# Two heads' attention scores issued alternately in pairs, with their value products and endings reordered

## What is computed

```python
def banded_attention(q, k, v, slopes, sinks, max_delta, dist):
    # blocks of 128 queries against the previous and the own block of 128 keys
    s = jnp.einsum("nbqgrd,nbkgd->nbgrqk", qb, kk).astype(jnp.float32) * (hd ** -0.5)
    p, lse = masked_softmax(s + bias, valid[:, None, None], sink)
    o = jnp.einsum("nbgrqk,nbkgd->nbqgrd", p.astype(v.dtype), vv)
# mixer A: 8 heads of 64 features, three groups (window, dilation) = (128,1), (512,4), (2048,16);
#   the groups of a head are combined by their softmax denominators
# mixer B: 8 query heads on 2 kv heads, window 128, with a sink added to the denominator
# h = RMSNorm(x); q, k (normed per head), v, gates z and g come from h @ w_in
# y = x + W_out( sig(g_A) * (A * silu(z_A)) @ P_A + sig(g_B) * (B * silu(z_B)) @ P_B )
```

## Time and profile before

| | us |
|---|---|
| median of 3 runs | 2293.25 |
| lowest and highest of them | 2286.2, 2364.95 |
| profiled execution | 2286.36 |
| its span, core 6, the slowest | 2284.7 |
| spans of the other cores | 2268.4 to 2282.2 |

### The profile page before, as it was taken

How to read it: one execution, slowest core, us unless ns; L and a number is a source line. 1 busy time by engine, 2 the same in 40 slices (tenths; PEclk the granted TensorE clock), 3 DMA queues, 4 the chain that set the end, 5 groups by cost and what they waited for, 6 DMA issues and landing times.

```text
span 2284.7 us, 43874 instructions; the slowest of 8 cores (2268.4 to 2284.7 us)
## 1 busy us (share of the span) xinstructions
PE 1885.7 (83%) x14352; PEld 1075.0 (47%) x14352; DVE 1256.1 (55%) x1948; ACT 1223.1 (54%) x2190; POOL 430.2 (19%) x519
## 2 busy tenths in 40 slices
PE   3676676799698987989869898877786999999995
PEld 1453453465465554655545554433343445444442
DVE  3454255455355563555625555576576577677773
ACT  3544365577376873768737686786798211111110
POOL 0032101112112131121311212322222111111111
PEclk8798888899899998999979998799898999999998
DMA  6498753489655896659965598679555658777764
GB/s 174 127 227 205 147 163 108 146 175 182 161 173 152 187 172 184 152 144 190 170 164 169 140 193 176 142 155 178 137 155 134 175 172 234 221 211 208 195 184 132
DMA packets 133998, 389.20 MB, mean 170 GB/s; under 512 B 15488, under 2 KB 87696, under 8 KB 129520
## 3 DMA queue, kind: packets, MB, share of 16 engines
q10 hardware_dynamic: 5680, 178.06, 31.6%
q1 hardware_dynamic: 97024, 119.95, 19.2%
q0 software_dynamic: 31072, 88.39, 18.6%
HBM read 363.23 MB, written 230.06 MB: 260 GB/s over the span
## 4 chain that ended last, share of the span: by engine, by line
PE 56%; ACT 13%; DMA 11%; issue 8%; DVE 7%; POOL 1%; ACTq 1%; another core or an unknown queue 1%; SPq 0%; DVEq 0%; POOLq 0%
PE ps L53 56%; ACT nl L53 6%; DMA xT<-scr_x 4%; DMA sa<-ra 3%; ACT sq L53 2%; ACT expt L53 2%; DMA rw<-win 2%; DVE pt L53 2%; ACT ld L53 2%; ACT rb L53 1%; DVE tt L53 1%; DVE ra L53 1%; DVE rd L53 1%; DMA rb<-xh 1%; DVE rb L53 1%
## 5 line engine op out<-in xcount | busy, mean ns | idle before, releaser
L53 PE MATMUL ps<-xT,rw 128*128 128x512 bf16 x2496 | 658.9, 399 | 38.1 <-DMA xT<-scr_x 34.4
L53 DVE TENSOR_TENSOR pt<-expt,mask 128x512 bf16<-128x512 f32 x512 | 386.5, 769 | 265.9 <-ACT expt L53 241.9
L53 ACT ACTIVATE expt<-ps 128x512 f32<-128x512 f32 x576 | 333.3, 596 | 130.8 <-PE ps L53 113.0
L53 PEld LDWEIGHTS ps<-xT,rw 128*128 128x128 bf16 x2496 | 248.3, 104 | 287.2 <-issue 82.7
L53 PE MATMUL ps<-ra,rd 64*128 64x128 bf16 (+2 forms) x1792 | 281.9, 281 | 24.7 <-ACT expt L53 12.7
L53 ACT ACTIVATE sq<-ps 128x512 bf16<-128x512 f32 x257 | 149.3, 581 | 240.7 <-PE ps L53 240.6
L53 PE MATMUL ps<-rw,xT 128*128 128x128 bf16 x3328 | 238.6, 234 | 20.1 <-DMA rw<-win 13.4
L53 ACT ACTIVATE nl<-ps,epsS 128x512 f32<-128x512 f32 x257 | 175.1, 681 | 148.3 <-PE ps L53 144.5
L53 PEld LDWEIGHTS ps<-rw,xT 128*128 128x128 bf16 x3328 | 226.8, 124 | 29.3 <-issue 23.2
L53 PEld LDWEIGHTS ps<-ra,rd 64*128 64x128 bf16 (+1 forms) x1792 | 127.8, 103 | 197.4 <-issue 132.4
L53 ACT ACTIVATE nl<-nl 128x512 f32<-128x512 f32 (+1 forms) x321 | 200.8, 626 | 29.5
(11 more groups left out here) (134 smaller groups left out, 2209.4 us busy)
## 6 DMA issues: line engine op xcount, KB each, us to landing
xT<-scr_x SPq DMA_DIRECT2D x40, 1024.0 KB, 12.0
sa<-ca ACTq DMA_DIRECT2D x32, 1020.0 KB, 9.1
ra<-ca POOLq DMA_DIRECT2D x48, 512.0 KB, 6.5
rw<-win POOLq DMA_DIRECT2D x78, 256.0 KB, 17.2
rb<-x SPq DMA_DIRECT2D x32, 512.0 KB, 5.2
rb<-xh SPq DMA_DIRECT2D x16, 512.0 KB, 8.3
scr_x<-xT POOLq DMA_DIRECT2D x8, 1024.0 KB, 8.6
scr_ab<-ra SPq DMA_DIRECT2D x64, 128.0 KB, 5.4
```

The costliest lines, as they stand in the source:

```text
L53: return lambda eng: getattr(eng, name)(*args, **kwargs)
```

## The change

1. `pair_heads` reorders `A`: within each group the tiles of head 0 and head 1 alternate. Every buffer that a group reads counts as read until the group's last tile.
2. `s` is split into its single matmuls and `s_post` (`Exp` and mask product). `do_tile` now handles two tiles: first `pv` and `fin` of all tiles that are open (the pair before), then the score matmuls of the two tiles alternately, head 0, head 1, head 0, ..., then both `s_post`. `LAG` is gone; one pair is open at most.
3. The planner asks for two credits and two available tiles, and the credit may grow to 4.
4. `finish_a` and `finish_b`: at once only DVE's sum or copy of the whole bank (128 partitions) into `TT`, for each head. The rest (ACT `Ln`, `Ln`, `Exp`, POOL, store) goes to a list `late` and is issued at the end of the next projection unit, behind that unit's tiles. In mixer B the `Ln` now reads `TT`, and the last POOL product is two of 64 partitions in place of one of 128.
5. Three tiles of their own (`OB`, 6 KB a partition) take the outputs that mixer B staged in `TT`.

```diff
+    OB, b_OB = tiles("ob", 3, [128, 512], F32)
...
-        def s():
-            stb = rST.next()
-            for ks, kap, qb, qap, c0, n in mms_s:
-                S.op(PE, lambda e: e.matmul(PS[stb][:, c0:c0 + n], lhsT=kap[rows, :], rhs=qap[rows, :], start=True, stop=True),
-                     reads=[ks.buf] + qb, writes=[b_PS[stb]])
+        def s_mm(m):
+            if "st" not in box:
+                box["st"] = rST.next()
+            stb = box["st"]
+            ks, kap, qb, qap, c0, n = m
+            S.op(PE, lambda e: e.matmul(PS[stb][:, c0:c0 + n], lhsT=kap[rows, :], rhs=qap[rows, :], start=True, stop=True),
+                 reads=[ks.buf] + qb, writes=[b_PS[stb]])
+
+        def s_post():
+            stb = box["st"]
...
+    def pair_heads(n0):
+
+        seg = A[n0:]
+        m = len(seg) // 2
+        A[n0:] = [t for p in zip(seg[:m], seg[m:]) for t in p]
+        for x in K1S + V1S + K2S + V2S + K3S + V3S:
+            if x.rd >= n0:
+                x.rd = len(A) - 1
...
         def fin(h):
             def f():
-                if h == 0:
-                    ts["t"], ts["l"] = rTT.next(), rLD.next()
-                ti, li = ts["t"], ts["l"]
-                ub, R, X = (UA, H0, H1) if h == 0 else (UB, H1, H0)
-                S.op(ACT, lambda e: e.activation(out=LD[li][R, :], in_=PS[ub][X, :], func=AF.Ln, bias=skW[X, c:c + 1]), reads=[b_PS[ub]] + C, writes=[b_LD[li]])
-                S.op(DVE, lambda e: e.tensor_copy(out=TT[ti][R, :], in_=PS[ub][R, :]), reads=[b_PS[ub]], writes=[b_TT[ti]])
+                flush_late(1)
+                ub = UA if h == 0 else UB
+                ti = ts[h] = rTT.next()
+                S.op(DVE, lambda e: e.tensor_copy(out=TT[ti][:, :], in_=PS[ub][:, :]), reads=[b_PS[ub]], writes=[b_TT[ti]])
                 if h == 1:
...
+                    late.append((cur[0], rest))
...
     def do_tile():
-        A[state["a"]].s()
-        state["a"] += 1
-        while state["pv"] < state["a"] - LAG:
+        while state["pv"] < state["a"]:
             do_pv()
+        t0, t1 = A[state["a"]], A[state["a"] + 1]
+        for f0, f1 in zip(t0.s, t1.s):
+            f0()
+            f1()
+        t0.s_post()
+        t1.s_post()
+        state["a"] += 2
+
+    def flush_late(keep):
+        while len(late) > keep:
+            late.pop(0)[1]()
...
-            acc = min(acc + rate, 3.0)
-            while acc >= 1 and avail > 0:
+            acc = min(acc + rate, 4.0)
+            cur[0] = i
+            while acc >= 2 and avail > 1:
                 do_tile()
-                avail -= 1
-                acc -= 1
+                avail -= 2
+                acc -= 2
+            while late and late[0][0] < i:
+                late.pop(0)[1]()
```

More of the change, by code:

```diff
@@ L425, in build_program, with __init__ @@
     class AT:
-        def __init__(self, after, s, pv, fin=None):
-            self.after, self.s, self.pv, self.fin = after, s, pv, fin
-    M, A = [], []
+        def __init__(self, after, s, s_post, pv, fin=None):
+            self.after, self.s, self.s_post, self.pv, self.fin = after, s, s_post, pv, fin
+    M, A, late, cur = [], [], [], [0]
     Wt = {}
@@ L442, in proj_mms @@
         return [first] + [(lambda k=k: mm(k)) for k in range(1, 8)]
-    out_tiles = {"a": (KF, b_KF, rKF, KO, b_KO, rKO, VO, b_VO, rVO), "b": (TT, b_TT, rTT) * 3}
+    out_tiles = {"a": (KF, b_KF, rKF, KO, b_KO, rKO, VO, b_VO, rVO), "b": (OB[0:1], b_OB[0:1], Rot([0]), OB[1:2], b_OB[1:2], Rot([0]), OB[2:3], b_OB[2:3], Rot([0]))}
     def norm_unit(ck, ncols, rhs_fn, rb, gcol, outs, slots=(), kout=None, step=None):
@@ L767, in pv @@
                      reads=[vs.buf, b_PT[pi]], writes=[b_PS[ub]])
-        A.append(AT(after, s, pv, fin))
+        A.append(AT(after, [(lambda m=m: s_mm(m)) for m in mms_s], s_post, pv, fin))
         for x in [m[0] for m in mms_s] + [m[0] for m in mms_v]:
@@ L817, in f, with rest @@
                 if h == 1:
+                    late.append((cur[0], rest))
+            def rest():
+                if True:
                     t0, t1, li, ai = ts[0], ts[1], rLD.next(), rAS.next()
@@ L841, in f @@
-                if h == 1:
[L842 to L847, removed]
+                flush_late(1)
@@ new lines, in f, with rest @@
+                ub = UA if h == 0 else UB
+                ti = ts[h] = rTT.next()
+                S.op(DVE, lambda e: e.tensor_copy(out=TT[ti][:, :], in_=PS[ub][:, :]), reads=[b_PS[ub]], writes=[b_TT[ti]])
+                if h == 1:
+                    late.append((cur[0], rest))
+            def rest():
+                t0, t1, li, ai = ts[0], ts[1], rLD.next(), rAS.next()
+                for t, R, X in ((t0, H0, H1), (t1, H1, H0)):
+                    S.op(ACT, lambda e: e.activation(out=LD[li][R, :], in_=TT[t][X, :], func=AF.Ln, bias=skW[X, c:c + 1]), reads=[b_TT[t]] + C, writes=[b_LD[li]])
+                S.op(ACT, lambda e: e.activation(out=LD[li][:, :], in_=LD[li][:, :], func=AF.Exp, scale=-1.0), reads=[b_LD[li]], writes=[b_LD[li]])
+                S.op(POOL, lambda e: e.tensor_tensor(out=LD[li][:, :], in0=LD[li][:, :], in1=SZ[zi][:, :], op=ALU.mult), reads=[b_LD[li], b_SZ[zi]], writes=[b_LD[li]])
+                for t, R in ((t0, H0), (t1, H1)):
+                    S.op(POOL, lambda e, t=t, R=R: e.tensor_tensor(out=AS[ai][R, :], in0=TT[t][R, :], in1=LD[li][R, :], op=ALU.mult),
+                         reads=[b_TT[t], b_LD[li]], writes=[b_AS[ai]])
+                S.dma(SP, lambda e: e.dma_start(out=scr_ab[gw, :, 4 + c, :], in_=AS[ai][:, :]), reads=[b_AS[ai]], writes=[b_ab[gw][4 + c]], semowner=b_AS[ai])
@@ L941, in build_program @@
             for r0 in range(0, 16, 4):
+                n0 = len(A)
                 for h in (0, 1):
@@ L945, in build_program @@
                               lambda r: (lambda ps: ps[:, 128 * r:128 * r + 128]), started, evac_g3(h, r0))
+                pair_heads(n0)
             qz_rd["q3"] = len(A) - 1
@@ L1420, in load_w @@
         S.dma(POOL, lambda e: e.dma_start(out=WB[slot].rearrange("p a b -> p (a b)"), in_=win_d[ck[1]]), writes=[b_WB[slot]], semowner=b_WB[slot])
-    LAG = 3
     n_units = sum(u.copyw for u in M)
@@ L1445, in force @@
             do_pv()
+        flush_late(0)
     dfr, dfr2 = [], []
```

## The result

The changed kernel takes 2451.5 us (median of 4 runs, 2448.2 to 2458.5) against 2291.0 for the kernel before (median of four runs: the three of the table above and one more): ratio 1.071, 95% interval 1.067 to 1.075. It is 7% slower, outside the predicted range. The profiled execution took 2458.5 us, and its slowest core is core 4; rows of the changed kernel are of that core where no other is named.

What follows compares the result with a forecast made beforehand. PE was taken to bound mixer A and ACT mixer B; 145 us saved against 139 added gave net -6 on the profiled 2286.4, so 2280 us, no change that could be told from none (chance 0.48), range 2210 to 2345.

Steps and rivals of the forecast that it cites:

- saved in mixer B: Mixer B: 8 of 26 us counted for switches and overlap, 20 (0 to 26) for waits for `Exp` and `TT` ending.
- What bounds each stage: PE bounds mixer A (busy 92%); ACT bounds mixer B (44.8 of 50 us in its undisturbed stretch).
- Switches and overlap, 77 us in mixer A: Fewer switches between 64-row and 128-row work and overlapping head scores save 0.40 us a pair, 192 pairs: 77 (36 to 96).
- Waits for squares, 40 of 64 gone: Mixer A: two thirds of PE's 63.6 us of waits for squares go, as ACT is freed: 40 saved (0 to 64).
- Waits in mixer A: 25 + 16 + 46 + 19 = 106: Mixer A, added: pairs with no projection unit before products, pairs with one, copies at group ends, the moved rest.
- the moved rest (19): Mixer A: `Ln`, `Ln`, `Exp` in one block before the next unit's `Ln`, 32 times 0.6, add 19 us (0 to 58).
- In mixer B ACT is the bound, so 0: Mixer B: pairs with one projection unit between scores and products add no wait; those with none were priced 2.3 us each.
- Clock, 10 us (-5 to 40): Many short waits in mixer A lower PE's clock by 0.02 to 0.04, adding 10 us.
- The new ending in mixer B, 0: Mixer B: `Ln` reading `TT` in place of the bank at 0 (-6 to 6); POOL's 45 us more hidden (0 to 10).
- second rival: Slower: PE waits for mask products after nearly each mixer A pair and its clock falls; +62, 2348 us; chance 0.20.
- third rival: Heads don't overlap when issued alternately: 0.19 in place of 0.40 us a pair, 40 less saved, 2320 us; chance 0.05.
- The signs: Right if mixer A's mask-product wait reaches 80, squares under 70, PE busy falls 100, passes stay 130 us; others marked rivals.

Runs made afterwards that it cites:

- e1: The changed kernel with two pairs open in place of one; ratio 1.001 (0.997 to 1.005) to the kernel before; some of its outputs are wrong.
- e9: The kernel before with alternating pairs, two open, and the new ending one unit later, all in mixer A only, plus extra buffers; 2257 us, ratio 0.985.
- e10: The kernel before with only mixer A's ending changed (rest one unit later), single tiles, LAG 3, extra buffers; 2273 us, ratio 0.991 to the kernel before.
- e6: The kernel before with both endings in the new form, rest one unit later, single tiles, LAG 3, a fourth gate buffer; ratio 1.008 to the kernel before.
- e3: The changed kernel with a pair's scores issued head 0 first, then head 1, not alternately; ratio 1.073 to the kernel before.

## Why the prediction was wrong

The sum again, term by term, against what the runs show. Savings are read from e1 against the kernel before, waits from the changed kernel against e1 (stages of the table):

| us | priced | shown |
|---|---|---|
| saved in mixer A | 77 + 40 = 117 | 41 (39 in e9) |
| added in mixer A, with the clock | 16 + 25 + 46 + 19 + 10 = 116 | 97 |
| saved in mixer B | 8 + 20 = 28 | -25 |
| added in mixer B | 23 | 73 |
| before and behind | 0 | 10 |

- **What bounds each stage.** Right for mixer A by busy shares, but PE bound it only while three tiles were open. For mixer B "ACT bounds that stage" was right of the kernel before and, as the step below shows, no reason to price a wait at 0.
- **Switches and overlap, 77 us in mixer A: the first step that failed.** Right in PE's busy time (76). But the sum took it for time one for one, and as time it was worth 20, with the lag restored (e10 to e9); 53 us went into new waits for squares. My reading, not tested by itself: less work for the busiest engine is not paid out where the next one, ACT, is busy two thirds of the stage and gets its work in bursts.
- **Waits for squares, 40 of 64 gone.** Too much: on core 0 of mixer A they fell from 71.9 to 57.0 us, 15. The part of it that was the ending's is real, though: e10 alone brings them to 33.6 and mixer A 19 us down. With the 77 that makes 117 us priced as saved, and some 40 shown: 76 of the whole error of 171.
- **Waits in mixer A: 25 + 16 + 46 + 19 = 106.** The size was right. Core 0 has 79.5 us of waits for mask products and 34.5 for `ACT nl`, all of them before product matmuls, the first six of them a few us behind a group's two copies: 114. In detail it was not: the moved rest (19) saves instead of costing.
- **The second step that failed: "In mixer B ACT is the bound, so 0", for the pairs with one unit between.** That sentence took ACT's full queue as given. But ACT is full only as long as PE is ahead of it. With one pair open the products wait behind norm, gate and copies (4.55 us in the timeline above), and the scores wait behind the products, so ACT runs dry. Priced at 0, with 23 for the ten pairs that have no unit between, the wait for the lag cost mixer B 73 us, which e1 gives back. It puts 50 of the whole error here; with the ending (below) mixer B, priced at 5 us gained, lost 98, over half of it.
- **Clock, 10 us (-5 to 40).** Too low: PE's busy time for the same matmuls is 41 us over e1's in mixer A, at the upper bound, and 28 in mixer B, where nothing was priced. (Busy time runs to a matmul's modelled end, so a part of that may be the ends that waits lay bare.) The same 2496 projection matmuls of 512 columns are busy 691 us against 659, those for the sum of squares 104 against 99. That is 37 us over the whole span on these two groups alone, at a clock of 0.880 against 0.917:

```profile
L53 PE MATMUL ps<-xT,rw 128*128 128x512 bf16 x2496 | 690.8, 419 | 13.8 <-DMA xT<-scr_x 8.1 <-DVE rd L53 2.9 <-DVE sq L53 2.5
L53 PE MATMUL ps<-sq,bonesB 128*128 128x512 bf16 x252 | 104.1, 413 | 90.2 <-ACT sq L53 89.8 <-issue 0.2
```

  In the kernel before, the lag alone moves the clock: 0.861 with LAG 1, 0.916 with LAG 2, 0.920 with 3. It is not the lag alone in every run: e1 waits 5.7 us for mask products and has 0.911, LAG 2 waits 111.8 and has 0.916. The rule that I cited from the Trainium skill ("TensorE: Matmul & The Clock Gate", section "A second HAM failure mode: psum-queue depth-cycling") gave the direction. By that rule short idles make the clock swing between its two levels. The trace agrees, with 1.00 before and 0.50 behind the 4.55 us wait above, and 0.887 for 0.920 over the cores. That the cause is the cycling through banks, no run shows.
- **The new ending in mixer B, 0.** The third step that failed. It costs 30 us there by itself (e6), in a form that was priced at 0 for `Ln` from `TT`, hidden for POOL's halves and not priced for DVE's copy of the whole bank. In the changed kernel ACT waits 24.8 us for `TT` with this `Ln`, and only 2.8 with mixer A's.
- **Rivals.** The second was the true one, in kind: many waits for mask products (87 in mixer A, with 192 pairs, and 38 in mixer B, with 64), and a lower clock with them. Its place was put in mixer A and its price at 62; it was 98 in mixer B and 56 in A. It had 0.20.
- **Overlap (third rival).** Rightly held unlikely: eight scores take 0.47 us. But e3 shows that the alternate order has no part in it.
- **The signs.** In mixer A the waits for mask products (80.8) and for squares (57.9) came out as named for the forecast, yet a pass took 151 us and not 130, and PE's busy time fell by 17 and not by 100. For the second rival the clock came (0.91, named under 0.92) and the busy share nearly (0.81, named under 0.8). That the waits in A had the size named, and the time was still 56 us longer, is the saving that didn't come.

## What to carry to other kernels

The depth of a software pipeline is measured in time: the way through the other engines' queues, not the sum of their durations, against the work that PE can issue in between. Here the sum of durations was 2.7 us, and the way through the queues in the step shown 6.8. The kernel before shows how steep the edge is, 0, 2 and 18% for three, two and one open tile. Before pricing a wait at nothing because another engine is the bound, ask whether that engine will still be fed while the wait lasts; in this ring of three engines with one item in flight none was busy above 65%. And a saving in the busiest engine's work is a saving in time only as far as the next engine's work comes earlier too: here 76 us of work gave 20 us.

A change with several parts should be tried part by part and stage by stage. Here mixer A's ending (0.9%) and pairs with two open in mixer A (0.6% more) pay; all parts together, in both mixers and with one open pair, cost 7%.

## What the hardware showed beyond expectation

- Score matmuls of 64 rows on different halves of the partitions run side by side whether issued alternately or one tile behind the other: eight of them take 0.41 us to the next projection either way, and e3's ratio equals the changed kernel's within 0.2%. In the kernel before, the place with three tiles together had shown the same.
- An `Ln` over 64 x 512 elements takes 719 ns out of SBUF with a bias from a tile, 683 ns out of a PSUM bank with the same bias, and 628 ns out of SBUF without a bias tile.
- With one open tile PE's granted clock fell to 0.79 in mixer B while every engine was busy under 65%; beside it stand, over the whole run, 236 waits for mask products of 1.9 us on average.
